# A two-block network on one core: modulation products moved from VectorE to ScalarE and GpSimd, a norm in halves, one root between the blocks, and two reordered loops

## The reference

```
mod = silu(c) @ mod_w + mod_b            # per layer: six rows of 1024 (shift, scale, gate, twice)
h   = rms_norm(x, g) * (1 + scale) + shift
# layer 1: RWKV-7 time mix of h (16 heads of 64, a recurrence over 512 tokens in 8 chunks)
# layer 2: forgetting attention; its K, V from a modulated norm of x of its own ("kv")
x   = x + (1 + gate) * y
h   = rms_norm(x, g) * (1 + scale) + shift
x   = x + (1 + gate) * (square(relu(h @ w_up)) @ w_down)        # MLP, width 4096
# after both layers: x = rms_norm(x, final_g)                   # input of the second block
# second block: h = rms_norm(x, g_mix) * (1 + sc1) + sh1, then
#   gated delta rule (8 heads of 128, gates b, a from h), latent attention, 16 experts, final norm
```

## Time and profile before

| | us |
|---|---|
| median of three runs | 3843.91 (3842.46 to 3846.12) |
| the profiled execution's own time | 3858.12 |
| its span, first to last instruction | 3856.3 |
| TensorE busy | 3546.2 (92%) |
| VectorE, ScalarE, GpSimd busy | 1406.1, 736.9, 389.2 |
| mean granted TensorE clock | 0.957 of full |

### The profile page before, as it was taken

How to read it: one execution, slowest core, us unless ns; L and a number is a source line. 1 busy time by engine, 2 the same in 40 slices (tenths; PEclk the granted TensorE clock), 3 DMA queues, 4 the chain that set the end, 5 groups by cost and what they waited for, 6 DMA issues and landing times.

```text
span 3856.3 us, 54440 instructions
## 1 busy us (share of the span) xinstructions
PE 3546.2 (92%) x24280; PEld 2184.1 (57%) x24280; DVE 1406.1 (36%) x2523; ACT 736.9 (19%) x1452; POOL 389.2 (10%) x301
## 2 busy tenths in 40 slices
PE   6699998899999999999997999998988999899998
PEld 2256666488886446688885466666433444443443
DVE  4533334187743004288632445454012210211111
ACT  1123333111002114211002222232102220200001
POOL 0210101022102000022104000010000001200000
PEclk7899999899999899999997999998899999999999
DMA  8310100255552120156422211010020113399997
GB/s 295 92 34 19 31 10 26 88 164 176 174 153 66 55 77 23 33 164 186 142 78 55 55 34 30 28 34 2 33 71 21 33 44 134 123 406 409 409 409 280
DMA packets 352746, 452.62 MB, mean 117 GB/s; under 512 B 18624, under 2 KB 258496, under 8 KB 352256
## 3 DMA queue, kind: packets, MB, share of 16 engines
q1 hardware_dynamic: 352512, 449.13, 34.1%
HBM read 444.87 MB, written 4.19 MB: 116 GB/s over the span
## 4 chain that ended last, share of the span: by engine, by line
PE 82%; DVE 8%; ACT 4%; DMA 4%; issue 1%; POOL 1%; SPq 0%; POOLq 0%; DVEq 0%; ACTq 0%
PE bank L79 82%; DVE A L70 3%; ACT A L87 2%; DVE SM L76 2%; DMA A<-in_w_up 1%; DVE A L76 1%; ACT SM L87 1%; DMA W<-in_mlp_up 1%; ACT H L87 1%; POOL SM L70 1%; DMA W<-in_w_up 0%; ACT A L86 0%; DVE X L76 0%; SPq L93 0%; DVE H L70 0%
## 5 line engine op out<-in xcount | busy, mean ns | idle before, releaser
L79 PE MATMUL bank<-A 64*64 64x64 f32 (+7 forms) x13408 | 1035.1, 261 | 89.8 <-ACT A L87 42.5
L79 PEld LDWEIGHTS bank<-A 64*64 64x64 f32 (+3 forms) x13408 | 814.1, 149 | 329.2 <-issue 129.0
L79 PE MATMUL bank<-A,W 128*128 128x512 f32 (+4 forms) x2336 | 836.3, 512 | 36.3 <-DMA W<-in_rw_g 18.4
L79 PE MATMUL bank<-H,W 128*128 128x512 f32 (+1 forms) x1776 | 691.8, 544 | 25.1 <-ACT H L87 9.5
L79 PEld LDWEIGHTS bank<-A,W 128*128 128x128 f32 (+3 forms) x2336 | 431.4, 190 | 383.2 <-issue 300.3
L79 PEld LDWEIGHTS bank<-H,W 128*128 128x128 f32 x1776 | 338.8, 194 | 342.7 <-issue 314.1
L87 ACT ACTIVATE A<-bank 128x512 f32<-128x512 f32 (+4 forms) x547 | 244.6, 451 | 1470.3 <-PE bank L79 1461.4
L79 PE MATMUL bank<-A,H 128*64 128x512 f32 (+1 forms) x1096 | 281.0, 595 | 11.9 <-ACT H L87 8.1
L70 DVE TENSOR_TENSOR A<-bank,A 128x256 f32<-128x256 f32 (+2 forms) x315 | 145.7, 476 | 391.4 <-PE bank L79 383.6
L70 POOL TENSOR_TENSOR A<-A 128x512 f32<-128x512 f32 (+1 forms) x104 | 146.0, 1413 | 1145.0 <-ACT A L87 440.0
L79 PE MATMUL bank<-W,H 128*64 128x512 f32 (+3 forms) x952 | 217.5, 492 | 21.3 <-ACT mods L87 12.3
(11 more groups left out here) (167 smaller groups left out, 2389.1 us busy)
## 6 DMA issues: line engine op xcount, KB each, us to landing
W<-in_mod_w SPq DMA_DIRECT2D x48, 1024.0 KB, 7.6
A<-in_w_gate SPq DMA_DIRECT2D x47, 1024.0 KB, 18.5
A<-in_w_up SPq DMA_DIRECT2D x42, 1024.0 KB, 18.6
A<-in_w_down SPq DMA_DIRECT2D x40, 1024.0 KB, 18.7
W<-in_mlp_up SPq DMA_DIRECT2D x64, 512.0 KB, 5.4
W<-in_mlp_down SPq DMA_DIRECT2D x128, 256.0 KB, 4.0
W<-in_w_mod SPq DMA_DIRECT2D x24, 1024.0 KB, 5.9
W<-in_w_down SPq DMA_DIRECT2D x24, 1024.0 KB, 18.5
```

The source lines that it names most:

```text
L79: return self.e.matmul(o, l, r, start=start, stop=stop, skip_group_check=True)
```

## The change

- `load`, `sp_mod`: the mod loads beside the MLPs have the kind "ma", and their slots are let go by ScalarE.
- `dv_mod` beside the MLPs is replaced: ScalarE makes the eight products of a group (copies with a scale), GpSimd adds them up, VectorE only adds the bias at the end (`dv_mod_row`).
- MLP norm: root, multiplication and modulation by token halves, over ScalarE, VectorE and GpSimd. Slice 0 takes its products in the order 1, 2, 3, 5, 6, 7, 4, slice 16 in the order 1, 2, 3, 6, 7, 5, 4.
- kv norm and the norm between the blocks: GpSimd adds one tile of squares less, TensorE takes it by a product of its own.
- Between the blocks: h of the second block needs one root alone, that of sum (s x)²/1024 + 1e-12, with s² = sqrt of (g² + 1e-6) in `geps`, which enters as the scale of the squares. R1_ for the final x is made from squares that GpSimd makes and adds, after the gates. `pe_gates2` stands inside head 0's fetch, whose four results go to banks 0 to 3.
- Recurrence: fetch in six pieces of four products; u of the next level at the end of a level's last step.

```diff
+        def ac_mod_products(ac, key, n, cc, earlier=None):
+            for g in range(n // 512):
+                for hf in range(2):
...
+                    for j in range(4):
+                        t = 4 * hf + j
+                        if t == 0:
+                            dst = mod_acc(g)
...
+                        else:
+                            dst = sqb[:, (t % 2) * 512:(t % 2) * 512 + 512]
+                            if t >= 3:
+                                ac.wait_ge(s_gp, ngp["ma", key, g, t - 2])
...
+                        m = ac.act(dst, v[:, j, :], COPY, scale=cact[:, cc + t:cc + t + 1])
+                        if j == 3:
+                            nac.mark_next("free", "ma", key, g, hf)
+                        m.then_inc(s_ac, nac("ma", key, g, t))
+                    yield
+                yield
+            yield
+        def gp_mod_sums(gp, key, n):
+            for g in range(n // 512):
+                for t in range(1, 8):
+                    gp.wait_ge(s_ac, nac["ma", key, g, t])
+                    gp.wait_ge(s_gp, ngp.n)
+                    gp.tt(mod_acc(g), mod_acc(g), sqb[:, (t % 2) * 512:(t % 2) * 512 + 512], ADD).then_inc(s_gp, ngp("ma", key, g, t))
+                    if t in (3, 7):
+                        yield
+                yield
+            yield
@@ pe_mod
+                if kind == "md":
+                    pe.wait_ge(s_dv, ndv["free", "md", key, g, 1])
+                else:
+                    pe.wait_ge(s_gp, ngp["ma", key, g, 7])
@@ pe_fetch
-            yield
+            yield from idle(2)
...
-                    if (8 * j + k) % 3 == 2:
-                        yield
-                        yield
-                        if 8 * j + k < 23:
-                            yield
+                    if k % 4 == 3:
+                        yield from idle(3)
@@ pe_scores
                 if lev == 1:
                     pe.wait_ge(s_dv, ndv["t", ct, 0])
-                else:
-                    pe.wait_ge(s_ac, nac["t", ct, lev - 1])
-                each(x, m8, T_).then_inc(s_pe, npe("u", ct, lev))
+                    each(x, m8, T_).then_inc(s_pe, npe("u", ct, lev))
                 yield
...
+                if lev < 5:
+                    pe.wait_ge(s_ac, nac["t", ct, lev])
+                    each(y, m8, T_).then_inc(s_pe, npe("u", ct, lev + 1))
                 yield
@@ MLP
+        FIRST = {0: (1, 2, 3, 5, 6, 7, 4), 16: (1, 2, 3, 6, 7, 5, 4)}
@@ ac_mlp
+            for n, s in enumerate((lo, hi)):
+                ac.act(rstd[:, s], BK[7][:, s], LN, scale=1.0 / D, bias=EPS).then_inc(s_ac, nac())
+                ac.wait_ge(s_ac, nac.n)
+                ac.act(rstd[:, s], rstd[:, s], EXP, scale=-0.5).then_inc(s_ac, nac("rstd", key, n))
+            for k in range(KT):
+                ac.wait_ge(s_dv, ndv["nx", key, k])
+                ac.act(h3[:, k, lo], h3[:, k, lo], ACT.Identity, scale=gs[:, k:k + 1], bias=sh[:, k:k + 1]).then_inc(s_ac, nac("nm", key, 0, k))
+            for k in range(4):
+                ac.wait_ge(s_gp, ngp["nx", key, k])
+                ac.act(h3[:, k, hi], h3[:, k, hi], ACT.Identity, scale=gs[:, k:k + 1], bias=sh[:, k:k + 1]).then_inc(s_ac, nac("nm", key, 1, k))
@@ gp_mlp
+            gp.wait_ge(s_ac, nac["rstd", key, 1])
+            for k in (4, 5, 6, 7, 0, 1, 2, 3):
+                gp.tt(h3[:, k, hi], x3[:, k, hi], rstd[:, hi], MUL).then_inc(s_gp, ngp("nx", key, k))
@@ dv_mlp
-            dv_norm(dv, "mlp" + l, g, mod[:, 32:40])
+            dv.wait_ge(s_ac, nac["rstd", key, 0])
+            for k in range(KT):
+                dv.tt(h3[:, k, lo], x3[:, k, lo], rstd[:, lo], MUL).then_inc(s_dv, ndv("nx", key, k))
+            for k in range(4, 8):
+                dv.wait_ge(s_gp, ngp["nx", key, k])
+                dv.ts(h3[:, k, hi], h3[:, k, hi], gs[:, k:k + 1], mod[:, 24 + k:25 + k], MUL, ADD).then_inc(s_dv, ndv("nm", key, 1, k))
@@ pe_gates, pe_gates2
-            pe.wait_ge(s_gp, ngp["sumg"])
-            pe.mm(BK[5][:, :], C("ones"), SQG, True, False)
-            pe.wait_ge(s_ac, nac["sqg"])
-            pe.mm(BK[5][:, :], C("ones"), sqb[:, 0:512], False, True).then_inc(s_pe, npe("ssg"))
...
             m.then_inc(s_pe, npe("gc"))
+            pe.wait_ge(s_gp, ngp["sumx"])
+            pe.mm(BK[6][:, :], C("ones"), SQG, True, True).then_inc(s_pe, npe("ssx"))
@@ ac_gates
             ac.act(EG, GCs, EXP).then_inc(s_ac, nac("eg"))
+            ac.wait_ge(s_pe, npe["ssx"])
+            ac.act(R1_, BK[6][:, :], LN, scale=1.0 / D, bias=EPS).then_inc(s_ac, nac())
+            ac.wait_ge(s_ac, nac.n)
+            ac.act(R1_, R1_, EXP, scale=-0.5).then_inc(s_ac, nac("r1"))
             ac.act(BE, ba[:, :, 0, :], ACT.Sigmoid).then_inc(s_ac, nac("be"))
@@ gp_gates
+            gp_squares(gp, "final1")
+            gp.wait_ge(s_pe, npe["pr", "1", 30, 4])
+            for n in range(KT):
...
+                gp.tt(SQG if n == 0 else V2_, x3[:, k, :], x3[:, k, :], MUL).then_inc(s_gp, ngp())
+                if n:
+                    gp.wait_ge(s_gp, ngp.n)
+                    gp.tt(SQG, SQG, V2_, ADD).then_inc(s_gp, ngp() if n < 7 else ngp("sumx"))
...
             for k in range(KT):
                 gp.wait_ge(s_dv, ndv["nx", "mix2", k])
+                gp.wait_ge(s_ac, nac["r1"])
                 gp.tt(x3[:, k, :], x3[:, k, :], R1_, MUL).then_inc(s_gp, ngp())
@@ pe_dfetch
-                pe.wait_ge(*left[0])
+                pe.wait_ge(*left[b])
+                if hd == 0 and i == 3:
+                    pe_gates2(pe)
```

More of the change, by code:

```diff
@@ L273, in load @@
                 sp.wait_ge(s_dv, ndv[("free",) + before])
+            elif before is not None and before[0] == "ma":
+                sp.wait_ge(s_ac, nac[("free",) + before])
             elif before is not None:
@@ L357, in pe_mod @@
+        def pe_mod(pe, key, n, cc, bc, on_pe=(), after=None, kind="md"):
             if after is not None:
@@ L415, in program, with ac_squares @@
         EPS = mods[:, 223:224]
-        def ac_squares(ac, key, n):
+        def ac_squares(ac, key, n, gain=None):
             k = ORDER[key][n]
@@ L422, in ac_squares @@
             await_x(ac, key, k)
-            ac.act(SQA if n == 0 else sqb[:, (n % 2) * 512:(n % 2) * 512 + 512], x3[:, k, :], SQUARE).then_inc(s_ac, nac("sq", key, n))
+            dst = SQA if n == 0 else sqb[:, (n % 2) * 512:(n % 2) * 512 + 512]
+            ac.act(dst, x3[:, k, :], SQUARE, scale=1.0 if gain is None else gain[:, k:k + 1]).then_inc(s_ac, nac("sq", key, n))
+        LAST = {k: 2 if k in ("kv", "final1") else 1 for k in SOURCE}
         def gp_squares(gp, key):
-            for k in range(1, 7):
+            for k in range(1, KT - LAST[key]):
                 gp.wait_ge(s_ac, nac["sq", key, k])
@@ L1228, in pe_seven @@
             pe.wait_ge(ring.sems[k], there)
-            for p in SEVEN:
+            for p in FIRST.get(i, SEVEN):
                 if first and g:
@@ new lines, in both @@
+            def both():
+                for i in range(32):
+                    if 1 <= i <= 16:
+                        relu(i - 1)
+                    if i < 16 or i % 4 == 3:
+                        g = i if i < 16 else 16 + (i - 16) // 4
+                        if g:
+                            ac.wait_ge(s_dv, ndv["ua", l, g - 1])
+                        ac.wait_ge(s_pe, npe["pr", l, i, 1])
+                        ac.act(UA, BK[BANK[1]][:, lo], COPY).then_inc(s_ac, nac("r1", l, g))
+                    yield
+                    yield
@@ new lines, in ac_mlp, with gp_mlp, both @@
+            woven(both(), *streams)
+        def gp_mlp(gp, l, *streams):
+            key = "mlp" + l
+            gp_squares(gp, key)
+            gp.wait_ge(s_ac, nac["rstd", key, 1])
+            for k in (4, 5, 6, 7, 0, 1, 2, 3):
+                gp.tt(h3[:, k, hi], x3[:, k, hi], rstd[:, hi], MUL).then_inc(s_gp, ngp("nx", key, k))
+            def both():
+                yield
+                yield
+                for j in range(16):
+                    for t in (j, j + 16):
+                        gp.wait_ge(s_ac, nac["up", l, t])
+                        gp.tt(hid[:, t, :], hid[:, t, :], hid[:, t, :], MUL).then_inc(s_gp, ngp("sq", l, t))
+                    if j % 4 == 3:
+                        c = j // 4
+                        K1, K2 = slice(4 * c, 4 * c + 4), slice(16 + 4 * c, 20 + 4 * c)
+                        gp.wait_ge(s_gp, ngp.n)
+                        gp.tt(hT2[:, K1, :], hid[:, K2, hi], hid[:, K1, hi], SUB).then_inc(s_gp, ngp())
+                        gp.wait_ge(s_gp, ngp.n)
+                        gp.tt(hT2[:, K1, :], hT2[:, K1, :], hid[:, K1, lo], ADD).then_inc(s_gp, ngp("hT2", l, c))
+                    yield
+                    yield
+            woven(both(), *streams)
@@ L1887, in pe_dfetch @@
                         m.then_inc(s_pe, npe("dq", hd, i))
-                        left[0] = (s_ac, nac["dq", hd, i])
+                        left[b] = (s_ac, nac["dq", hd, i])
```

(11 more changed lines are left out.)

164 lines of the change are left out of this document (81 added, 83 removed).

## The result

| | before | after |
|---|---|---|
| median, us (ten runs each) | 3845.68 (3841.94 to 3853.34) | 3833.29 (3828.26 to 3840.36) |
| ratio, 95% interval | | 0.9966 (0.9955 to 0.9976) |
| profiled execution, own time | 3858.12 | 3833.65 |
| its span | 3856.3 | 3831.8 |

The change makes the kernel 12.4 us faster (0.34%), where 40 us were forecast. The profiled execution of before lay 12.4 us above its median, that of after 0.4. About twelve of the 24.5 us between the two spans are therefore no work of the change: they show in unchanged code, 3.6 us in the attention, 5.6 in the last rounds of the delta rule and 3.2 behind them.

The account below looks back on a forecast made before the run. TensorE holds 82% of the chain, so only ending its waits and the lower clock after them pays. Terms -20 - 11 - 9 - 2 - 1 + 3 = -40 gave 3818 us profiled, 3804 us median; range 3786 to 3830, held at about 0.8.

Parts of the forecast that it names:

- rivals 2 and 3: 2: recurrence keeps its waits, -8 instead of -20, 3816 us, chance 0.15; 3: MLPs give nothing, 3824 us, chance 0.12.
- Recurrence: Delta-rule rounds: regrouped fetch and earlier product u remove TensorE's waits on VectorE; -20 us, ends -8 and -25.
- what loses its cover is the end of the round: Recurrence steps 19 to 24 hold no fetch piece; some three more copies are bare, +1.0 us a round.
- twenty products instead of fifteen: Recurrence, middle round: twenty products now precede the bonus product, so its 1.3 us wait goes too.
- MLP products moved: Modulation products to ScalarE, sums to GpSimd; turn waits go: -11 us first MLP, -9 second; ends together -28 and 0.
- I also keep 1 in each for VectorE held off by GpSimd: Both MLPs: 1 us of gain held back in each because GpSimd's port lock delays VectorE.
- these stay: 3.0 for 3.0: MLPs: GpSimd's late groups make TensorE wait as much as the three modulation waits before, 3.0 us.
- rival 4: GpSimd's additions pace the MLPs, deciding from 1.8 us each; at 2.0 us the kernel is slower, 3864 us; chance 0.06.
- Norms: MLP norm in halves: comes out 1 us earlier per norm, -2 us; ends -5 and +3.
- KV norm: KV norm: one GpSimd addition of 1.27 us leaves the path, a TensorE pass comes in; -1 us.
- Between the blocks: Earlier start ends in a 16 us TensorE wait on GpSimd's queue before DG_, then half clock; +3 us, ends -12 and +8.
- the signs named beforehand: Expected rounds about 61 us, no turn wait over 2; wrong if rounds stay 64, MLP GpSimd waits exceed 10, DG_ ready.

Follow-up runs that it names:

- the six traces with this code: Traces of the changed kernel and of five follow-up edits of it that leave the MLP code alone; second MLP 414.5 us in the changed kernel, 411 to 413 in the five.
- the five other traces: Traces of five follow-up edits of the changed kernel that leave the MLP code alone; slice 1 takes 18.1 to 19.6 us in the first MLP, 16.6 to 18.3 in the second.
- the kernel with both edits taken back: Changed kernel with fetch again in eight pieces of three and powers read just ahead of their masks; 3840.13 us, ratio 0.9984.
- narrow additions: Changed kernel with GpSimd's seven group 0 additions, in kv and second-MLP modulation, on one column instead of 512; 3822.78 us, ratio 0.9936.

## Why the prediction failed

The sign was right, the size not: -12.4 us instead of -40, and just outside the range (3833.3 against 3830). What came out is nearly rivals 2 and 3 together, which the text had priced only apart.

- **Recurrence**, -20 forecast, 8.4 us measured. The step that failed is "what loses its cover is the end of the round". The waits on VectorE went as I said, through the early powers: alone they bring a middle round from 64.0 to 62.5 us. But eight pieces of three cover more steps than six of four. I looked only at what a piece of four would hide, and not at which two steps lose their piece: steps 3 and 12, where ScalarE's tanh and small copy are late by 1.3 and 1.7 us. So the four middle rounds, forecast 12.8 us shorter, came out 2.2 longer (64.2, 64.2, 64.2 and 65.8 us for 64.0). The rounds ahead of them, forecast 9.7 us shorter, gave 9.5, and those behind, forecast 0, gave 1.1: there the mechanism held. A second step failed too, that twenty products instead of fifteen would end the 1.3 us ahead of the bonus product: with fours alone the wait stays at 1.3, and the early powers are what shortens it. The reason that I gave for 20 instead of 22, product u waiting for the copy of T, showed nowhere as a wait of its own.
- **MLP products moved**, -11 and -9 forecast, +0.8 and -1.6 measured on the MLPs' lengths (-1.6 to -4.7 for the second over the six traces with this code). The -11 was added up wrongly as well: 4.1 + 2.0 + 5.8, less the 2 and the 1 kept back, is 9. The turn went as forecast in the second (slice 16: 23.3 to 13.0 us). Two steps failed. "I also keep 1 in each for VectorE held off by GpSimd": this measured 6.7 and 6.5 us, in slice 1 (5.1 to 6.6 and 3.6 to 5.3 in the five other traces). I had held the slowed sums against the 12.1 us of a running slice; in the first slices VectorE has four x differences of 128x1024 before them and starts late. And "these stay: 3.0 for 3.0": the late rows measured 7.6 and 3.5 us of waits, one of them 5.7 us at the first MLP's turn, with low clock behind it; having them asked for later gave 10.9 and 6.0 us. The price of one addition was mis-sized with it, 1.27 us taken, 1.43 measured in the mean and 1.77 in the burst. The mean stays well under the 1.8 us from which rival 4 was to decide; only seven of the 117 additions in the first MLP took longer, and GpSimd did not pace the MLPs.
- **Norms**, -2 forecast: the wait before the first product went from 3.20 to 2.50 us in the first MLP, and slice 0 from 14.9 to 15.6 us in both. No gain from the halves is shown. **KV norm**: 1.2 us, as forecast.
- **Between the blocks**, +3 forecast, +0.9 measured: 2.0 us less to the product behind the wait and 2.9 us more behind it, at the lower clock (2 to 4 forecast for that). The mechanism held as written: VectorE's first normalised tile 4.7 us after the MLP's last product (2050.1), then r1 behind the gates, GpSimd's queue, and a wait of 18.0 us where 16 were forecast. VectorE's eight multiplies took 12.1 us, as I took them with all eight held off.
- The carry-over from the profiled execution to the median was right in size: 14.2 us taken, 12.4 measured on ten runs.

Of the signs named beforehand, three failed at once: rounds at 64 us, slice 16 of the first MLP, and waits on GpSimd that sum to 11.1 us.

## What to carry to other kernels

When pieces of filler work are regrouped between dependent steps, list for each step what it waits for and which piece covers it, before and after. Fewer, larger pieces close the waits that one was looking at and open others. When work goes to a second elementwise engine, look at the place where the first one has no slack, mostly the start of a stage. A burst there cost its full slowing and the spell at low clock after it; a slice later it cost next to nothing. A consumer of such work should ask for it a slice later than the arithmetic says.

## What the runs showed of the hardware

- The slowing of VectorE and GpSimd is mutual, and larger than the earlier trace rows had led me to expect: GpSimd's additions went from 1.27 us to 1.77 in the mean and 2.08 at most, VectorE's operations with two operands from SBUF from 0.69 to 1.64 or 1.75 and from 1.22 to 2.29 us. It also held up a tiny scaling of 128x8, 1.23 us beside the burst and 0.16 with narrow additions.
- An addition of GpSimd on 128x1 took 0.69 us, one on 128x512 1.27: with one column for 512 over half of its price stays.
- TensorE's clock was at 0.50 for 6.8 us around and behind the waits of 3.4 and 5.7 us, from 0.6 and 1.4 us before their ends on. Behind the waits of 2.6 us it was 0.66 to 0.71 over the next 5 us in all five rounds of the kernel with fetch in fours and late powers, and 0.66 behind the one such wait of the kernel with both edits taken back, but 1.00 behind the same wait of the kernel before. Once, in the changed kernel, it was 0.54 behind a wait of 1.3 us, at which it mostly stayed at 1.00. What decides between these was not tried.
